# One search moved across the attention of a two-layer streaming encoder: seven bits ahead of the first recurrence tile instead of four, none beside the attention

## The chip, the cores and the metric

The kernel runs on one core of one Trainium2 chip. The metric is the device time of one execution in microseconds; the median of three executions of the kernel before is 2104.66 us.

## The reference, cut to what matters

The model has two layers. Each layer normalises its tokens, projects them, and runs four groups of heads over them: HGRN2 and retention (two gated linear recurrences), forgetting attention ("fox") and DSA sparse attention. It is done for 1040 prompt tokens and for 32 tokens of a running stream with 1024 cached rows. Only the DSA selection matters for the change: each query keeps the 256 keys with the highest index score.

```python
def _dsa_attend(q, k, v, iq, ik, iw, cid_q, cid_k, k_top):
    sc = jnp.einsum('bqhd,bkd->bqhk', iq, ik).astype(jnp.float32)
    score = jnp.einsum('bqhk,bqh->bqk', jax.nn.relu(sc), iw.astype(jnp.float32)) * IDX_SCALE
    adm = cid_k[None, :] <= cid_q[:, None]
    score = jnp.where(adm[None], score, -jnp.inf)
    kk = min(k_top, k.shape[1])
    _, sel = lax.top_k(score, kk)
...
    s = jnp.einsum('bqhd,bqsd->bqhs', q, k_sel).astype(jnp.float32) * (HD_C ** -0.5)
    s = jnp.where(valid[:, :, None, :], s, -jnp.inf)
    p = jax.nn.softmax(s, axis=-1).astype(v.dtype)
    return jnp.einsum('bqhs,bqsd->bqhd', p, v_sel)
```

## The kernel before, in words

The prompt is cut into nine tiles of 128 tokens (tile 0 is short and holds the stream's 32 tokens and the 16 meta tokens). A layer is one block of five instruction streams (PE, ACT, DVE, POOL, SP), each written out in a fixed order; they meet only at semaphores, and an engine that waits holds back all that is written behind the wait. The stages of a layer, for DVE:

1. **Norm, first projection and index scores.** DVE accumulates the index scores of eight units: the stream ("s", 32 x 1056) and the prompt tiles 2 to 8 (128 rows by 320, 448, ... 1088 keys), L1766.
2. **The selection's threshold.** No sort is used. The 256th largest score of each row is found bit by bit, 31 bits from bit 30 down. `search(n)` (L1810) makes n *steps* of it; a bit is `SEARCH` = 10 steps: one that sets the trial threshold `theta` (L1817), eight counts of the scores at or above it, one for each unit (`count_one`, L1783), and one that takes the bit over into `prefix` (L1822, L1824, L1826). A count writes the comparison's result, which nobody reads, to a scratch tile (`relu[0]`) and the sum into `cnt8`. Of the 31 bits four are made ahead of the first recurrence tile (`search(4 * SEARCH)`), then 7 steps in the first recurrence tile and 15 in each other, then what is left but two bits after the last tile (`search(31 * SEARCH - LATE - at_search[0])`), while PE still projects.
3. **The recurrence**, nine tiles of a chain between PE, ACT, DVE and POOL. For a tile POOL first turns and scales the loaded rows (`rotate` and `forget`, L2115 to L2136), ACT takes the logarithm, PE sums it up (L1031) and transposes (L1038), and DVE copies that out of PSUM (`x_qke`, L1840); all later work of the tile on DVE stands behind this copy. Between these PE fills its time with matmuls of the projections (L927), by a planner's table that the change does not touch.
4. **The attention**, 74 jobs in the order of the list `AJ`: 37 of fox, then 37 of DSA; a job is one head of one tile (the stream's is one job for all heads). PE makes the scores (L1221), DVE takes each row's maximum (`mneg`, L2067), ACT the exponentials (L1645), PE transposes these (L1235), ACT and DVE copy them out (L1378), PE multiplies with the values (L1271) and transposes back (L1279), and DVE scales (L1991).
5. The output projection, norm and residual (L1291, L2235).

In the attention DVE has *extra steps* besides: the last two bits of the search (`LATE`, 20 steps), then `penalise`, six steps for each of the eight units, which turn threshold and scores into an additive mask `pen` (0 or -1e30) that the DSA jobs add to their scores. By line: L1953 restores the sign, L1955 and L1956 compare above and equal, L1958 and L1959 rank the equal ones by a scan, L1961 and L1963 join, L1965 writes the mask. The extra steps stand in DVE's stream just ahead of the wait for a job's scores; how many ahead of which job comes from `steps_by`: in proportion to the jobs' lengths up to the job of DSA tile 6, and no later than `due`, four jobs ahead of the first job that reads the unit's mask. The 20 + 48 steps before are all made by job 61. The first late step waits for the last four stores of the projection (`st_out`), because from there on the scratch and masks lie where these stores read.

## Time and profile before

| | us |
|---|---|
| median of 3 runs | 2104.66 (2103.86 to 2107.75) |
| the profiled execution, its own time | 2108.83 |
| its span | 2107.0 |
| PE matmul busy | 1923.3 (91%) |
| DVE busy | 1387.2 (66%) |
| ACT busy | 736.7 (35%) |
| POOL busy | 254.4 (12%) |

Layer 1 fills the span up to about 1053 us, layer 2 the rest; they run the same instructions. In layer 1 the search begins at 182 us, the recurrence has DVE from 244 to about 545 us, the attention lasts from about 649 to 910 us, the output follows. In layer 2 all lies some 1051 us later. Granted clock 0.988 of full speed over the span.

### The profile page before, as it was taken

The numbers are of one execution on the slowest core, as the hardware profiler recorded it, in microseconds if no ns is written. First come the engines' busy times: TensorE is split into PE (matmuls) and PEld (weight loads), VectorE is DVE, ScalarE is ACT, GpSimd is POOL, SyncE is SP. The second block draws the span as 40 slices with busy tenths as digits, with TensorE's granted clock in tenths as the row PEclk, the third lists the DMA queues.
The fourth block names the chain that finished last, engine by engine and source line by source line (L and its number), as shares of the span: only waits on it lengthen the run. The fifth ranks groups of instructions, "written<-read, shape, count | busy, mean of one in ns | idle before, by whom it ended". The sixth has DMA issues, their size and how long they took to land. (4 is left out here: it accounts for less than half of the span.)

```text
span 2107.0 us, 27058 instructions
## 1 busy us (share of the span) xinstructions
PE 1923.3 (91%) x9670; PEld 1073.9 (51%) x9690; DVE 1387.2 (66%) x2961; ACT 736.7 (35%) x1678; POOL 254.4 (12%) x361
## 2 busy tenths in 40 slices
PE   7999999999998888999779999999999987889997
PEld 6434466555445556544364344665554455565443
DVE  4469398989796666542234693989888956674322
ACT  4451233423113444433244512434331134344332
POOL 0000223322100000001100002234221000000011
PEclk9999999999999999999979999999999999999999
DMA  7102232130513002224251022331314130122242
GB/s 245 59 22 78 70 106 86 61 103 28 154 38 73 14 14 91 87 99 147 107 175 61 23 75 75 103 99 46 103 43 139 38 76 11 34 70 88 99 149 105
DMA packets 151156, 173.44 MB, mean 82 GB/s; under 512 B 71392, under 2 KB 106848, under 8 KB 150832
## 3 DMA queue, kind: packets, MB, share of 16 engines
q1 hardware_dynamic: 122960, 134.34, 20.4%
q10 hardware_dynamic: 28064, 37.38, 5.0%
q8 instruction: 78, 1.28, 0.2%
q14 instruction: 54, 0.44, 0.1%
HBM read 114.94 MB, written 62.24 MB: 84 GB/s over the span
## 5 line engine op out<-in xcount | busy, mean ns | idle before, releaser
L927 PE MATMUL ps<-wring,xnT_arena 128*128 128x512 f32 (+2 forms) x2304 | 920.3, 541 | 0.0
L927 PEld LDWEIGHTS ps<-wring,xnT_arena 128*128 128x128 f32 x2304 | 403.1, 191 | 355.7 <-issue 338.7
L1783 DVE TENSOR_SCALAR_CACHE_REDUCE arena<-arena,theta 32x1056 bf16<-32x1056 f32 x496 | 461.3, 979 | 2.3
L1414 ACT COPY arena<-ps 128x512 f32<-128x512 f32 (+3 forms) x144 | 75.3, 523 | 447.7 <-PE ps L927 414.1
L1291 PE MATMUL ps<-wring,xnT_arena 128*128 128x512 f32 x512 | 222.8, 593 | 0.0
L2067 DVE TENSOR_REDUCE mneg<-ps 128x1 f32<-128x192 f32 (+9 forms) x148 | 113.9, 770 | 84.6 <-PE ps L1223 82.1
L1291 PEld LDWEIGHTS ps<-wring,xnT_arena 128*128 128x128 f32 x512 | 95.9, 190 | 114.8 <-issue 114.8
L1067 PEld LDWEIGHTS ps<-arena 128*128 128x128 f32 x488 | 68.7, 190 | 103.5 <-DVE arena L1890 75.1
L1067 PE MATMUL ps<-arena 128*128 128x128 f32 x488 | 79.5, 286 | 35.9 <-DVE arena L1890 35.7
L2235 POOL TENSOR_TENSOR arena<-arena 128x1024 f32<-128x1024 f32 (+1 forms) x16 | 35.4, 2213 | 584.0 <-DVE arena L2008 397.5
L1378 ACT COPY xnT_arena<-ps 128x512 f32<-128x512 f32 (+3 forms) x84 | 39.0, 464 | 181.8 <-PE ps L1235 139.1
L1221 PE MATMUL ps<-xnT_arena,arena 128*128 128x512 f32 (+4 forms) x240 | 86.3, 475 | 14.8 <-DVE xnT_arena L1378 13.2
L1221 PE MATMUL ps<-arena 128*128 128x512 f32 (+4 forms) x240 | 92.6, 473 | 7.8 <-DVE xnT_arena L1378 6.7
L1890 DVE TENSOR_TENSOR arena<-o_bc,arena 64x128 f32<-64x128 f32 x244 | 95.7, 392 | 3.8
L1645 ACT ACTIVATE arena<-ps,mneg 128x576 f32<-128x576 f32 (+5 forms) x84 | 80.9, 963 | 25.1 <-DVE mneg L2067 24.4
L1378 DVE COPY xnT_arena<-ps 128x512 f32<-128x512 f32 x104 | 61.2, 605 | 38.7 <-PE ps L1271 20.4
L1766 DVE SCALAR_TENSOR_TENSOR arena<-arena,iw 32x1056 f32<-32x1056 f32 (+7 forms) x64 | 63.7, 996 | 27.8 <-ACT arena L1477 25.7
L1235 PE MATMUL ps<-cf,arena 128*128 128x128 f32 (+2 forms) x596 | 79.1, 273 | 1.0 <-ACT arena L1645 1.0
L1872 DVE COPY_PREDICATED arena<-cm,ps 128x256 f32<-128x256 uint8 x122 | 63.5, 521 | 23.6 <-PE ps L1067 22.4
L1848 DVE TENSOR_TENSOR arena<-arena 128x256 f32<-128x256 f32 x122 | 76.2, 635 | 2.7
L1548 ACT ACTIVATE arena<-arena 128x128 f32<-128x128 f32 x122 | 37.7, 309 | 106.5 <-DVE arena L1848 100.1
L1235 PEld LDWEIGHTS ps<-cf,arena 128*128 128x128 f32 (+2 forms) x596 | 63.9, 136 | 18.9 <-issue 12.8
(271 smaller groups left out, 2468.0 us busy)
## 6 DMA issues: line engine op xcount, KB each, us to landing
projected<-arena ACTq DMA_DIRECT2D x130, 256.0 KB, 2.0
wring<-in_w_in SPq DMA_DIRECT2D x16, 1024.0 KB, 7.8
o_bc<-projected SPq DMA_DIRECT2D x36, 384.0 KB, 3.7
wring<-in_w_in SPq DMA_DIRECT2D x6, 2048.0 KB, 9.0
arena<-residual SPq DMA_DIRECT2D x17, 512.0 KB, 5.1
arena<-in_x_prompt SPq DMA_DIRECT2D x16, 512.0 KB, 5.0
wring<-in_w_out SPq DMA_DIRECT2D x8, 1024.0 KB, 6.1
residual<-arena SPq DMA_DIRECT2D x16, 512.0 KB, 2.7
```

The lines of the kernel that those rows point to most:

```text
L927: o = mm(bank(pbank(k), 0, w_), xnT[:, c, t * P:(t + 1) * P], w, start=(c == 0), stop=(c == CH - 1))
L1067: o = mm(bank(level_bank(k), 2 * n_ * g, 2 * n_), keys[:, g * P:(g + 1) * P], queries[:, g].rearrange("p e n -> p (e n)"), start=True, sto ...
L1221: o = mm(ps[:, col:col + w], qt[:, h, :], kt[:, h if m == "fox" else 0, key:key + w], start=True, stop=not adds, skip_group_check=True)
L1235: o = tr(ps[0:w, 512 * tbank[a] + P * i:512 * tbank[a] + P * i + P], pbuf((m, u, h))[:, col:col + w], C("ident"))
L1291: o = mm(bank(OUT_BANK[t] + half), yT[t % 2][:, c, :], wring[:, c * D + 512 * half:c * D + 512 * half + 512], start=(c == 0), stop=(c == C ...
L1378: copy(ptile[pt_of[m, u, h]][:, 4 * g * P:4 * g * P + size], bank(tbank[a], 0, size)).then_inc(te, 1)
L1414: nc.scalar.copy(stage[s][:, 0:wide], bank(pbank(k), 0, wide)).then_inc(p_ev, 1)
L1645: A(pbuf((m, u, h))[:, 0:hi - lo], ps[:, base + lo:base + hi], ACT.Exp, bias=mneg[:, s:s + 1], accum_out=rsum[:, s:s + 1]).then_inc(a_exp, 1)
L1783: V.tensor_scalar(cmp_out[0][r, (i % 2) * WMAX:(i % 2) * WMAX + uw[u]], score[u][r], th_, 0.0, op, ALU.add, accum_out=into[r, i:i + 1]).th ...
L1848: V.tensor_tensor(dl[k[1] % 2].rearrange("p (b s) -> p b s", s=size), bv, bv[:, :, size // 2 - 1:size // 2].broadcast_to([P, 2 * P // size ...
L1890: V.tensor_tensor(QL[k[1] % 2][r, :, e, :].rearrange("p g (b i) -> p g b i", i=size // 2), cut_(QKA[:, 0])[r, :, :, size // 2:], cut_(E[k[ ...
L2067: V.tensor_reduce(mneg[:, s:s + 1], ps[:, base + lo:base + hi], X, ALU.max, negate=True).then_inc(a_max, 1)
```

## The change

The search makes 70 steps ahead of the first recurrence tile instead of 40. Inside the recurrence nothing moves. After the last tile all the rest is made, 113 steps instead of 123, and none beside the attention. There only the 48 penalty steps are left, which the same rule now spreads over the same jobs. The wait for the last stores, with a product `thr8` of eight columns, now heads `penalise`, which is called ahead of every job, also with 0 steps; as long as no penalty step has been made (`at_pen[0] == 0`) each call makes both.

```diff
-                    cmp_out = [relu[0].bitcast(BF16)]
+                    cmp_out = relu[0].bitcast(BF16)
...
-                    search(4 * SEARCH)
+                    search(7 * SEARCH)
                     dve.wait_ge(x_split, 1)
...
                     head_squares(NT - 1)
-                    LATE = 2 * SEARCH
-                    search(31 * SEARCH - LATE - at_search[0])
+                    search(31 * SEARCH - at_search[0])
...
-                    def late_search(n):
-
-                        if at_search[0] == 31 * SEARCH - LATE:
+                    def penalise(n):
+
+                        if at_pen[0] == 0:
                             for j in jobs[-len(st_out):]:
                                 dve.wait_ge(st_out[st_out_slot[j]], st_out_at[j])
-                            cmp_out[0] = keep_equal
-                        search(n)
-                        if at_search[0] == 31 * SEARCH:
                             V.tensor_tensor(thr8, prefix.bitcast(F32), sg8, ALU.mult).then_inc(dve_own, one_more(own))
                             dve.wait_ge(dve_own, own[0])
-
-                    def penalise(n):
-
                         for _ in range(n):
...
-                    total = LATE + PEN_STEPS * len(UNITS)
-                    due = {job_no["dsa", u, 0] - 4: LATE + PEN_STEPS * (i + 1) for i, u in enumerate(PEN_ORDER)}
+                    total = PEN_STEPS * len(UNITS)
+                    due = {job_no["dsa", u, 0] - 4: PEN_STEPS * (i + 1) for i, u in enumerate(PEN_ORDER)}
...
-                            for _ in range(further(n)):
-                                if at_search[0] < 31 * SEARCH:
-                                    late_search(1)
-                                else:
-                                    penalise(1)
+                            penalise(further(n))
                             dve.wait_ge(a_sc, a_sc_at[key])
```

Only DVE's stream changes. Ahead of the first recurrence tile, DVE, the difference at the end of the fourth bit (`arena` holds the scores and the scratch, `sel` the counts):

```order
 L1824 TENSOR_SCALAR bitv<-sel 128x8
 L1826 TENSOR_TENSOR prefix<-prefix,bitv 128x8
+L1817 TENSOR_SCALAR theta<-prefix 128x8
+L1783 TENSOR_SCALAR arena,sel<-arena,theta 32x1056
+L1783 TENSOR_SCALAR arena,sel<-arena,theta 128x320
+L1783 TENSOR_SCALAR arena,sel<-arena,theta 128x448
+L1783 TENSOR_SCALAR arena,sel<-arena,theta 128x576
+L1783 TENSOR_SCALAR arena,sel<-arena,theta 128x704
+L1783 TENSOR_SCALAR arena,sel<-arena,theta 128x832
+L1783 TENSOR_SCALAR arena,sel<-arena,theta 128x960
+L1783 TENSOR_SCALAR arena,sel<-arena,theta 128x1088
```

A bit of these twelve instructions is added three times in each layer; behind the third stands, as before, the copy L1840 of the first recurrence tile.

DVE at the head of the attention, before (L2067 is a job's maximum, L1378 a copy of transposed exponentials, L1982 the stream's scaling):

```order
L2067 TENSOR_REDUCE mneg<-ps 128x1
L1817 TENSOR_SCALAR theta<-prefix 128x8
L2067 TENSOR_REDUCE mneg<-ps 128x1
L1378 COPY xnT_arena<-ps 128x512
L1378 COPY xnT_arena<-ps 128x128
L2067 TENSOR_REDUCE mneg<-ps 128x1
L1783 TENSOR_SCALAR arena,sel<-arena,theta 32x1056
L1783 TENSOR_SCALAR arena,sel<-arena,theta 128x320
L2067 TENSOR_REDUCE mneg<-ps 128x1
L1378 COPY xnT_arena<-ps 128x512
L1977 RECIPROCAL rinv<-rsum 128x1
L1982 TENSOR_SCALAR o_bc<-ps,rinv 32x64 x4
```

And in the changed kernel, whose lines here are numbered 7 to 11 lower (L1936 is `thr8`, L2056 the maximum, L1946 the first penalty step, L1948 and L1949 the second):

```order
L2056 TENSOR_REDUCE mneg<-ps 128x1
L1936 TENSOR_TENSOR sel<-prefix,sel 128x8
L1946 TENSOR_SCALAR arena<-arena,sel 32x1056
L2056 TENSOR_REDUCE mneg<-ps 128x1
L1378 COPY xnT_arena<-ps 128x512
L1378 COPY xnT_arena<-ps 128x128
L2056 TENSOR_REDUCE mneg<-ps 128x1
L1948 TENSOR_SCALAR arena,sel<-arena,sel 32x1056
L1949 TENSOR_SCALAR arena<-arena,sel 32x1056
L2056 TENSOR_REDUCE mneg<-ps 128x1
L1378 COPY xnT_arena<-ps 128x512
```

Penalty steps stand where search steps stood, from the third job on, and fewer of them; `thr8` stands ahead of each of the first three jobs.

## Rows read from the trace of the kernel before

**Rows 1.** Busy by stretch: us, PE, PEld, DVE, ACT, POOL, clock, DMA share, GB/s.
```profile
655.00:868.00 213.00, 180.15 (x1398) 123.21 (x1406) 142.51 (x289) 96.27 (x257) 0.71 (x2) 1.00 0.21 56
1706.00:1919.00 213.00, 179.47 (x1385) 122.90 (x1382) 141.60 (x289) 96.21 (x256) 0.19 (x1) 0.99 0.20 55
868.00:888.00 20.00, 19.35 (x136) 12.20 (x137) 8.47 (x16) 10.93 (x23) 0.00 (x0) 1.00 0.12 26
770.00:790.00 20.00, 14.27 (x116) 8.53 (x114) 14.04 (x25) 8.31 (x16) 0.00 (x0) 1.00 0.09 19
890.00:910.00 20.00, 14.87 (x117) 9.09 (x116) 10.84 (x19) 11.17 (x17) 0.00 (x0) 0.94 0.26 93
```

**Rows 2.** Timeline of DVE at the first recurrence tile: start, us, instruction, [idle before, releaser].
```profile
244.36 0.69 DVE L1840 COPY o_bc<-ps 128x512 f32<-128x512 f32 x1 [29.50 <-PE ps L1038]
...
1295.18 0.69 DVE L1840 COPY o_bc<-ps 128x512 f32<-128x512 f32 x1 [29.15 <-PE ps L1038]
```

**Rows 3.** Timeline of DVE in layer 1, where two bits of the search begin.
```profile
190.21 0.17 DVE L1817 TENSOR_SCALAR theta<-prefix 128x8 int32<-128x8 int32 x1
...
198.44 0.17 DVE L1817 TENSOR_SCALAR theta<-prefix 128x8 int32<-128x8 int32 x1
```

**Rows 4.** Timelines of POOL and PE ahead of the first recurrence tile, layer 1.
```profile
231.54 1.09 POOL L2115 TENSOR_TENSOR arena<-o_bc,cf 128x512 f32<-128x512 f32 x1 [60.22 <-DMA o_bc<-projected]
...
237.77 0.53 POOL L2161 MEMSET arena<- 128x512 f32 x1
...
238.42 1.14 PE L1031 MATMUL ps<-cf,arena 128*128 128x128 f32 x4 [2.36 <-ACT arena L1494]
```

**Rows 5.** Timelines of POOL and DVE in the second recurrence tile.
```profile
276.13 0.73 POOL L2146 TENSOR_TENSOR arena<-arena 128x256 f32<-128x256 f32 x1
...
246.14 0.90 POOL L2146 TENSOR_TENSOR arena<-arena 128x256 f32<-128x256 f32 x1
...
276.00 1.06 DVE L1783 TENSOR_SCALAR_CACHE_REDUCE arena<-arena,theta 128x832 bf16<-128x832 f32 x1
```

**Rows 6.** Timeline of DVE, first instruction behind the search's end in both layers.
```profile
649.41 1.46 DVE L1362 COPY xnT_arena<-ps 65x512 f32<-65x512 f32 x2 [5.29 <-PE ps L1137]
...
1699.96 1.46 DVE L1362 COPY xnT_arena<-ps 65x512 f32<-65x512 f32 x2 [5.31 <-PE ps L1137]
```

**Rows 7.** DVE's groups by line from 662 to 862: count | busy us, mean ns | idle before.
```profile
L1783 DVE TENSOR_SCALAR_CACHE_REDUCE arena<-arena,theta 32x1056 bf16<-32x1056 f32 (+7 forms) x16 | 15.4, 984 | 0.1
L1959 DVE TENSOR_TENSOR_SCAN arena<-cb,arena 32x1056 f32<-32x1056 bf16 (+7 forms) x8 | 13.6, 1704 | 0.0
...
L1961 DVE SCALAR_TENSOR_TENSOR arena<-arena,sel 32x1056 bf16<-32x1056 f32 (+7 forms) x8 | 7.9, 991 | 0.1
L1955 DVE TENSOR_SCALAR_CACHE_REDUCE arena<-arena,sel 32x1056 bf16<-32x1056 f32 (+7 forms) x8 | 7.9, 983 | 0.1
L1956 DVE TENSOR_SCALAR arena<-arena,sel 32x1056 bf16<-32x1056 f32 (+7 forms) x8 | 4.8, 604 | 0.0
L1953 DVE TENSOR_SCALAR arena<-arena,sel 32x1056 f32<-32x1056 f32 (+7 forms) x8 | 4.8, 600 | 0.1
...
L1963 DVE TENSOR_TENSOR arena<-arena 32x1056 bf16<-32x1056 bf16 (+7 forms) x8 | 4.3, 538 | 0.0
L1965 DVE TENSOR_SCALAR arena<-arena 32x1056 bf16<-32x1056 bf16 (+7 forms) x8 | 2.8, 350 | 0.2
```

**Rows 8.** Chain of waits, shares by line: 1700 to 1760, then 1760 to 1820.
```profile
by line: DMA gpre<-projected 15.0%; DVE arena L1783 12.3%; PE ps L1271 10.1%; PE ps L1221 8.2%; issue 7.8%; DVE mneg L2067 7.4%; PE ps L1260 7.2%; PE ps L1137 5.1%; DVE xnT_arena L1378 4.4%; PE ps L1235 4.4%; PE ps L1151 2.9%; DVE o_bc L199
...
by line: PE ps L1221 19.2%; PE ps L1271 18.6%; issue 13.3%; PE ps L1235 9.3%; DVE arena L1959 5.9%; DVE mneg L2067 5.7%; DVE xnT_arena L1378 3.4%; PE ps L1151 3.0%; PE ps L1279 2.6%; DVE arena L1961 2.2%; DVE o_bc L1991 1.5%; DVE arena L195
```

**Rows 9.** Last store of the projection, the stores' time to landing, first maximum.
```profile
648.61 0.33 ACTq L1420 DMA_DIRECT2D projected<-arena  x1
...
projected<-arena ACTq DMA_DIRECT2D x130, 256.0 KB, 2.0
...
657.24 1.26 DVE L2067 TENSOR_REDUCE mneg<-ps 128x1 f32<-128x1056 f32 x1 [3.13 <-PE ps L1223]
```

More of the change, by code:

```diff
@@ L1782, in count_one @@
                             dve.wait_ge(dve_own, counted[i % 2])
-                        V.tensor_scalar(cmp_out[0][r, (i % 2) * WMAX:(i % 2) * WMAX + uw[u]], score[u][r], th_, 0.0, op, ALU.add, accum_out=into[r, i:i + 1]).then_inc(dve_own, one_more(own))
+                        V.tensor_scalar(cmp_out[r, (i % 2) * WMAX:(i % 2) * WMAX + uw[u]], score[u][r], th_, 0.0, op, ALU.add, accum_out=into[r, i:i + 1]).then_inc(dve_own, one_more(own))
                         counted[i % 2] = own[0]
```

## The prediction

> **What bounds the kernel now.** I read the trace in four steps. First the busy time by stretch [rows 1]: over most of a layer PE is full, but in the attention, 655 to 868 us, it works 180.15 of 213 us and idles for 32.9 (33.5 in layer 2), and nobody else is full either: DVE works 142.5 us, ACT 96.3. Such a stage is bound by the chain from engine to engine: scores, maximum, exponentials, transposes, copies, values. A DVE instruction that stands ahead of a maximum can lengthen this chain although DVE has idle time elsewhere. Second DVE's timeline at the first recurrence tile [rows 2]: there DVE sits idle for 29.50 us in layer 1 and 29.15 us in layer 2, until a PE transpose of that tile is done. Third the end of the search, ahead of the attention: DVE is done with its search and waits another 5.3 us in both layers [rows 6], so what stands there is hidden behind PE. Fourth the chain of waits in the attention of layer 2 [rows 8]: the counts of the late search hold 12.3% of the first 60 us, which is 7.4 us; in the next 60 us the scan of the penalty steps holds 5.9%, 3.5 us. So the extra steps do stand on the path there, but by no means all the time.
>
> **Seven bits ahead of the recurrence: 0 us.** A bit takes 198.44 - 190.21 = 8.23 us from one theta to the next [rows 3]. Three added bits are 24.7 us in each layer, and the idle gap that they fall into is 29.50 and 29.15 us [rows 2]; 4.8 and 4.5 us of it are left. The copy L1840 starts when PE releases it, as before. Behind it everything on DVE keeps its place, since 30 added steps are three whole bits and the 15 steps of each tile fall on the same units. The cover is this gap; if the three bits took over 29.15 us, each us more would delay the first tile by one, in each layer. What the trace of before does not show is POOL's preparation of the tile running beside counts; that is the rival on the other side, below. Its bounds are 0 and 7.9 us a layer; I take 0, by the nearest row [rows 5].
>
> **Ten steps fewer behind the last tile: 0 us.** One bit, 8.2 us, leaves a stretch at whose end DVE waits 5.3 us for PE anyway [rows 6]. That wait grows to about 13.5 us and nothing starts earlier.
>
> **The wait for the stores moves from the third job to the first: 0 us.** The last store is issued at 648.61 and such stores land in 2.0 us at the median, so at about 651; the first maximum, behind which the wait cannot hurt, starts at 657.24 and has waited 3.13 us for PE itself [rows 9]. Six us are left. With thr8 it is made three times instead of once; thr8 is of the size of theta, 0.17 us [rows 3], and the first two fall into idle time ahead of jobs whose scores are late. At most 0.3 us a layer, taken as 0.
>
> **Two bits fewer beside the attention: the only term.** They are 2 x 8.23 = 16.5 us of DVE work a layer (the 16 counts alone are 15.4 us [rows 7]). The seven large lines of the penalty steps stay: 13.6 + 7.9 + 7.9 + 4.8 + 4.8 + 4.3 + 2.8 = 46.1 us [rows 7]. How much of 16.5 us of DVE work does the attention give back? I bound it by two readings.
> - From idle time. Of the 32.9 us that PE idles in 655 to 868, part would be there without any extra steps. Where DVE has none left, 868 to 888, PE idles 0.65 us of 20 [rows 1]; tile 8 of DSA, also without extra steps, idles 5.1 of 20, about as much as tile 8 of fox with them, 5.7 [rows 1]. So without extra steps the 213 us would idle some 193 x 0.65 / 20 + 5.1 = 11.4 us. The rest, 21.5 us, I put down to 46.1 + 16.5 = 62.6 us of extra steps: 0.34 us for each us. For 16.5 us that is 5.7 us a layer.
> - From the chain. Counts hold 7.4 us of it in layer 2 [rows 8]. Taking them away can't shorten this chain by more than that and its small neighbours, since behind the chain lies the next one, so 7.4 us is the upper end. The lower end is 0: DVE idles between the jobs, and a step can slide there.
>
> What speaks for less than 5.7 is where the work goes from. Not the first jobs are relieved but all of them, a little: by the rule for the steps 21 stand ahead of job 22 and its forerunners before (20 of the search, 1 penalty), and 14 penalty steps now. A unit's six steps are on average 1704 + 991 + 983 + 604 + 600 + 538 + 350 ns = 5.8 us [rows 7], so 14 of them are 13.5 us or more, against 17.2 before. Only 3 to 4 us are gone by there, the other 13 over jobs 23 to 61. And the new ones are longer: a scan of 1.7 us where counts took 1.0 [rows 7]. I take 5.0 us a layer, 10 us in all.
>
> **Sum.** Against the profiled execution, 2108.8 - 10 = 2098.8 us. That execution lies 4.2 us above the median of the runs shown; against this median, 2104.7 - 10 = 2094.7 us. Differences under 0.2%, 4.2 us here, are about what a measurement of this kernel can't tell from no change.
>
> **Rivals.** (a) *The attention gives back less than 2 us a layer*, because the longer penalty steps now sit in the small first jobs and the chain through PE is as late as the one through DVE. For it: DVE idles a third of the stage; tile 8 of fox and of DSA idle alike with and without extra steps [rows 1]. Against it: the counts' 12.3% on the chain [rows 8]. Time about 2102.5.
> (b) *It gives back all that the chain shows*, 7.4 us a layer and some of the small steps at the bits' ends: 15 to 16 us, time about 2089. For it: those rows. Against it: a chain names the last wait only, and the next one may lie a few tenths behind.
> (c) *POOL is held up ahead of the first tile, and the kernel gets slower.* In layer 1 POOL runs nine instructions from 231.54 to 238.30, and PE idles 2.36 us for their result (over ACT) at 238.42 [rows 4]: they are on the path. Before, DVE was silent there; now the seventh bit runs over them, from 244.36 - 29.50 + 2 x 8.23 = 231.3 to 239.5. If each of the eight that read had to wait for a count, on average 0.98 us [rows 7], that were 7.9 us a layer, 15.7 in all, and with the 10 us gained the time would be 2110.4. It decides from 0.63 us an instruction upward (8 x 0.63 = 5). Against it: L2146 took 0.73 us where it ran over a count that was on from 276.00 to 277.06, and 0.90 us at another place [rows 5]. No slowing by a count is seen.
> The Trainium skill, "SBUF — State Buffer", section "Who interferes with whom", calls the port pair that DVE and GpSimd share an exclusive lock, and says that the loser fully blocks. By this headline alone rival (c) would be the forecast, at 2110. The same section excepts the scalar form that also writes out its accumulator, which is what a count is; read so it gives 0, and the trace agrees, with 0.73 us.
> (d) *The change doesn't do what it says*: the order of DVE shows that it does; no chance is kept for it.
>
> **Chances.** The forecast, 3 to 6.5 us a layer, 0.60; (a) 0.15; (b) 0.20; (c) 0.05. So faster by over 0.2%: 0.60 + 0.20 = 0.80; within 0.2%: 0.15; slower: 0.05. The range leaves out (c) and the ends of (a) and (b): from 2086, a little below (b) at 2089 for what the small steps and the medians may add, to 2103, just above (a).
>
> **What the changed profile would show.** DVE's idle time ahead of L1840 falls from 29.50 and 29.15 to about 4.8 and 4.5 us, and L1840 starts at 244.4 and 1295 as before; POOL's nine instructions still take 6.8 us and PE's wait of 2.36 us stays. The recurrence is the same to a us. DVE's wait at the end of the search grows from 5.3 to about 13.5 us. The attention has no L1783, DVE works about 16 us less in it, and PE idles about 28 us instead of 33; each layer ends some 5 us earlier. I am wrong if the idle time ahead of L1840 vanishes and the copy comes late, if the attention's length stays though its DVE work is 16 us less (then the counts were covered), or if it shrinks by over 8 us a layer (then the chain's shares were too small a bound).

## The result, and the profile after

| | before | changed |
|---|---|---|
| median, us (20 runs of each) | 2108.60 (2103.42 to 2111.81) | 2112.36 (2105.76 to 2118.11) |
| changed / before | | 1.0023 (95%: 1.0013 to 1.0033) |
| the profiled execution, its own time | 2108.83 | 2109.71 |
| its span | 2107.0 | 2107.9 |
| mean granted clock | 0.9870 (89 runs, those beside the experiments) | 0.9822 (20 runs) |

The changed kernel is slower, by 0.23% or 4.9 us (the two medians alone lie 3.8 us apart, the two means 4.8). The forecast was 2094.7 us, 10 us faster. The sign was wrong.

The page of the changed kernel: PE is busy 8.5 us longer with the same matmuls (the trace of the kernel before lacks 20 of their records), DVE as long as before, since the bits have only moved.

```profile
span 2107.9 us, 27104 instructions
...
PE 1931.8 (92%) x9690; PEld 1077.8 (51%) x9690; DVE 1387.9 (66%) x2965; ACT 737.5 (35%) x1678; POOL 254.5 (12%) x361
```

**What came out as forecast.** DVE's timeline of the changed kernel at the first recurrence tile and behind the search (to be read against [rows 2, 6]):

```profile
241.64 0.69 DVE L1840 COPY o_bc<-ps 128x512 f32<-128x512 f32 x1 [2.02 <-PE ps L1038]
...
646.74 1.46 DVE L1362 COPY xnT_arena<-ps 65x512 f32<-65x512 f32 x2 [13.61 <-PE ps L1137]
...
1294.38 0.69 DVE L1840 COPY o_bc<-ps 128x512 f32<-128x512 f32 x1 [3.86 <-PE ps L1038]
...
1699.15 1.46 DVE L1362 COPY xnT_arena<-ps 65x512 f32<-65x512 f32 x2 [13.55 <-PE ps L1137]
```

The three bits fit into the gap: DVE is still released by PE, with 2.02 and 3.86 us to spare, and at the search's end it waits 13.6 us. POOL's nine instructions ahead of the first tile, now beside the seventh bit, and PE's wait for them (against [rows 4]):

```profile
230.48 1.10 POOL L2104 TENSOR_TENSOR arena<-o_bc,cf 128x512 f32<-128x512 f32 x1 [59.89 <-DMA o_bc<-projected]
...
232.71 0.73 POOL L2109 TENSOR_TENSOR arena<-arena 128x256 f32<-128x256 f32 x1
...
236.73 0.52 POOL L2150 MEMSET arena<- 128x512 f32 x1
...
237.38 0.68 PE L1031 MATMUL ps<-cf,arena 128*128 128x128 f32 x4 [2.05 <-ACT arena L1494]
```

From 230.48 to 237.25 are 6.8 us, as before. In layer 1 the copy starts 2.7 us earlier than in the kernel before. That is not the change: PE's L1031 took 1.14 us there before [rows 4] and takes 0.68 now, the granted clock from 238 to 242 being 0.57 then and 1.00 now, and in e1, with the same seven bits in front, the low clock and the late copy (243.85) are back. So the front and the tail show no cost; e1 tests it. The profiled pair differs by only 0.9 us in all because of such differences: its two attentions are 4.8 us longer, as the table below shows, and the rest is 3.9 us shorter, 2.7 of it at this place.

**Where the time went.** Lines of the changed kernel's attention carry lower numbers: L1946 to L1958 are the penalty steps, L1952 the scan, L2056 the maximum. DVE's groups by line from 659 to 862 (against [rows 7]) have no count left, and the maxima wait 37.7 us, where L2067 waited 23.9; the eight scans take 13.6 us as before:

```profile
L2056 DVE TENSOR_REDUCE mneg<-ps 128x1 f32<-128x64 f32 (+9 forms) x64 | 45.8, 716 | 37.7 <-PE ps L1223 36.5 <-DVE arena L1949 0.2
```

Busy time by stretch, attention of both layers (columns as in [rows 1]):

```profile
652.00:865.00 213.00, 182.69 (x1391) 124.05 (x1392) 125.52 (x249) 96.25 (x257) 0.72 (x2) 0.98 0.20 53
1705.00:1918.00 213.00, 182.96 (x1376) 125.12 (x1370) 125.24 (x248) 95.50 (x255) 0.19 (x1) 0.96 0.19 50
```

DVE works 17.0 and 16.4 us less, as forecast, and PE idles 30.3 and 30.0 us instead of 32.9 and 33.5. That looks like the forecast, and yet the stage is longer. The reason is the seventh figure: the clock was 1.00 and 0.99 there before and is 0.98 and 0.96 now. PE's extra busy time is not work, it is the same work at the lower level.

To see where the stage loses, I follow the maxima, which have the same order in every variant. DVE's timeline of the changed kernel; the widths name the jobs (1056: the stream, 576: a head of tile 4; jobs are counted from 0):

```profile
654.51 1.26 DVE L2056 TENSOR_REDUCE mneg<-ps 128x1 f32<-128x1056 f32 x1 [2.58 <-PE ps L1223]
...
672.32 2.33 DVE L1952 TENSOR_TENSOR_SCAN arena<-cb,arena 32x1056 f32<-32x1056 bf16 x1
674.69 0.76 DVE L2056 TENSOR_REDUCE mneg<-ps 128x1 f32<-128x576 f32 x1
...
681.30 0.76 DVE L2056 TENSOR_REDUCE mneg<-ps 128x1 f32<-128x576 f32 x1 [0.34 <-PE ps L1223]
...
782.25 1.26 DVE L2056 TENSOR_REDUCE mneg<-ps 128x1 f32<-128x1056 f32 x1 [2.36 <-PE ps L1223]
...
798.27 2.15 DVE L1952 TENSOR_TENSOR_SCAN arena<-cb,arena 128x960 f32<-128x960 bf16 x1
...
800.46 0.76 DVE L2056 TENSOR_REDUCE mneg<-ps 128x1 f32<-128x576 f32 x1
...
811.27 0.76 DVE L2056 TENSOR_REDUCE mneg<-ps 128x1 f32<-128x576 f32 x1 [0.93 <-PE ps L1223]
```

The same view and places in the kernel before:

```profile
674.91 0.68 DVE L1783 TENSOR_SCALAR_CACHE_REDUCE arena<-arena,theta 128x448 bf16<-128x448 f32 x1
675.52 0.75 DVE L2067 TENSOR_REDUCE mneg<-ps 128x1 f32<-128x576 f32 x1
...
680.67 0.76 DVE L2067 TENSOR_REDUCE mneg<-ps 128x1 f32<-128x576 f32 x1
...
785.73 1.26 DVE L2067 TENSOR_REDUCE mneg<-ps 128x1 f32<-128x1056 f32 x1 [2.38 <-PE ps L1223]
...
801.21 0.81 DVE L1959 TENSOR_TENSOR_SCAN arena<-cb,arena 128x320 f32<-128x320 bf16 x1
...
802.06 0.76 DVE L2067 TENSOR_REDUCE mneg<-ps 128x1 f32<-128x576 f32 x1
...
811.02 0.76 DVE L2067 TENSOR_REDUCE mneg<-ps 128x1 f32<-128x576 f32 x1 [0.74 <-PE ps L1223]
```

Subtracting the first maximum (654.51 now, 657.24 before) from each, and the same in layer 2:

| from the first maximum to | before, layers 1 / 2 | changed | difference |
|---|---|---|---|
| job 8, width 576 | 23.43 / 24.20 | 26.79 / 28.64 | +3.4 / +4.4 |
| job 37, width 1056 | 128.49 / 129.27 | 127.74 / 130.50 | -0.8 / +1.2 |
| job 45, width 576 | 153.78 / 154.56 | 156.76 / 159.54 | +3.0 / +5.0 |
| the output projection, L1301 | 250.6 / 252.6 | 252.6 / 255.4 | +2.0 / +2.8 |

So the attention does gain where it was to gain, 4.1 and 3.2 us between jobs 8 and 37 and 1.0 and 2.2 us at the end (of the 2.2, some 1.3 is the kernel before losing time at a low clock of its own, at 1900 to 1904). But it loses 3.4 to 4.4 us ahead of job 8 and 3.7 us in each layer in jobs 37 to 45. In both losing stretches a wide scan now stands ahead of a maximum of a small tile: the stream's, 2.33 us, ahead of job 6, where a count of 0.68 us stood; unit 7's, 2.15 us, ahead of job 41, where the scan of the narrowest unit stood, 0.81 us. Behind each PE waits, and then runs slow. PE's timeline of the changed kernel:

```profile
676.72 2.10 PE L1271 MATMUL ps<-xnT_arena 128*64 128x128 f32 x20 [3.10 <-ACT ptile L1378]
...
806.60 2.26 PE L1271 MATMUL ps<-xnT_arena,arena 128*64 128x128 f32 x20 [1.71 <-ACT xnT_arena L1690]
```

and of the kernel before:

```profile
677.55 1.46 PE L1271 MATMUL ps<-xnT_arena 128*64 128x128 f32 x20 [1.27 <-ACT ptile L1378]
...
807.89 1.46 PE L1271 MATMUL ps<-xnT_arena,arena 128*64 128x128 f32 x20 [1.40 <-ACT xnT_arena L1690]
```

The same twenty matmuls took 1.46 us before and take 2.10 and 2.26. Busy by stretch in the changed kernel shows the clock there:

```profile
677.00:680.00 3.00, 3.00 (x23) 1.82 (x19) 0.64 (x2) 0.27 (x1) 0.00 (x0) 0.55 0.00 0
...
807.00:810.00 3.00, 3.00 (x21) 1.82 (x17) 0.60 (x2) 0.27 (x1) 0.00 (x0) 0.50 0.00 0
1730.00:1734.00 4.00, 4.00 (x23) 2.30 (x20) 1.18 (x2) 0.27 (x1) 0.00 (x0) 0.50 0.01 4
```

Granted 0.50 to 0.55 is the 1.2 GHz level. In the kernel before, at these places:

```profile
677.00:681.00 4.00, 3.45 (x34) 2.57 (x35) 2.37 (x8) 1.14 (x7) 0.00 (x0) 1.00 0.00 0
808.00:812.00 4.00, 3.95 (x37) 2.85 (x37) 1.51 (x4) 0.94 (x5) 0.00 (x0) 1.00 0.00 0
```

The attention of the changed kernel has seven such falls in the profiled execution (three in layer 1, four in layer 2); the one before had one, at 1900 to 1904. The Trainium skill, "TensorE: Matmul & The Clock Gate", section "The HAM clock gate", says that the array's clock is gated by how busy PE has been of late, at half or at full rate. The trace agrees in kind: 0.55 behind a wait of 3.10 us, 1.00 where that wait was 1.27. But the clock is also 0.50 behind a wait of 1.71 us (after one of 1.07 us shortly before), and stays at 1.00 behind 1.40 (after 0.62), so the length of the last wait alone does not tell a fall.

The chain of waits of 1700 to 1760 (against [rows 8]) has lost the 12.3% of the counts and got PE's own lines in their place: L1221 went from 8.2 to 17.2%, L1235 from 4.4 to 8.1%, and the scan has come in.

```profile
by line: PE ps L1221 17.2%; DMA gpre<-projected 14.2%; PE ps L1271 10.7%; PE ps L1235 8.1%; issue 7.3%; PE ps L1260 7.2%; PE ps L1137 5.0%; DVE mneg L2056 4.4%; DVE arena L1952 3.8%; PE ps L1151 2.9%; DVE xnT_arena L1378 2.6%; PE ps L1279 2
```

**The theory.** The change is two edits. It takes two bits out of the attention, and it hands the 48 penalty steps, which stood ahead of jobs 22 to 61, to a rule that spreads them from the first job on. The first gains, the second loses more. Rivals: the seven bits in front (or POOL there) cost something after all; the repeated `thr8` costs; the counts were covered and nothing was gained. The scans of one unit after the other stood ahead of these jobs:

| unit | s | 4 | 5 | 6 | 2 | 7 | 3 | 8 |
|---|---|---|---|---|---|---|---|---|
| before, and e2 | 24 | 28 | 33 | 36 | 41 | 48 | 54 | 59 |
| changed | 6 | 15 | 23 | 29 | 34 | 41 | 51 | 58 |
| e3 | 11 | 17 | 22 | 28 | 34 | 48 | 53 | 59 |
| e11 | 26 | 30 | 34 | 37 | 46 | 53 | 58 | 63 |

### The profile page after: what moved, and what is told of

Its sections match the earlier page's. It is cut to its first block and busy times, and to the rows that moved or that the text cites. A ratio compares the mean times of both kernels' runs of the same rounds, so it can differ in the third digit from the quotient of the medians.

```text
span 2107.9 us, 27104 instructions
## 1 busy us (share of the span) xinstructions
PE 1931.8 (92%) x9690; PEld 1077.8 (51%) x9690; DVE 1387.9 (66%) x2965; ACT 737.5 (35%) x1678; POOL 254.5 (12%) x361
## 5 line engine op out<-in xcount | busy, mean ns | idle before, releaser
L2056 DVE TENSOR_REDUCE mneg<-ps 128x1 f32<-128x192 f32 (+9 forms) x148 | 114.0, 770 | 110.1 <-PE ps L1223 107.9
L1378 ACT COPY xnT_arena<-ps 128x512 f32<-128x512 f32 (+3 forms) x84 | 39.0, 464 | 199.5 <-PE ps L1235 153.7
L1221 PE MATMUL ps<-arena 128*128 128x512 f32 (+4 forms) x240 | 94.2, 481 | 8.8 <-DVE xnT_arena L1378 8.8
L1221 PE MATMUL ps<-xnT_arena,arena 128*128 128x512 f32 (+4 forms) x240 | 89.0, 488 | 9.3 <-DVE xnT_arena L1378 7.8
L1378 DVE COPY xnT_arena<-ps 128x512 f32<-128x512 f32 x104 | 61.3, 605 | 44.1 <-PE ps L1271 24.6
L1235 PE MATMUL ps<-cf,arena 128*128 128x128 f32 (+2 forms) x596 | 81.9, 280 | 0.5 <-ACT arena L1645 0.5
L1984 DVE TENSOR_TENSOR o_bc<-ps,rinv 128x128 f32<-128x128 f32 (+1 forms) x72 | 20.9, 291 | 86.8 <-PE ps L1279 85.6
L1235 PEld LDWEIGHTS ps<-cf,arena 128*128 128x128 f32 (+2 forms) x596 | 66.5, 140 | 18.4 <-issue 12.1
```

The costliest lines, as they stand in the source:

```text
L1221: o = mm(ps[:, col:col + w], qt[:, h, :], kt[:, h if m == "fox" else 0, key:key + w], start=True, stop=not adds, skip_group_check=True)
L1235: o = tr(ps[0:w, 512 * tbank[a] + P * i:512 * tbank[a] + P * i + P], pbuf((m, u, h))[:, col:col + w], C("ident"))
L1378: copy(ptile[pt_of[m, u, h]][:, 4 * g * P:4 * g * P + size], bank(tbank[a], 0, size)).then_inc(te, 1)
L2056: V.tensor_reduce(mneg[:, s:s + 1], ps[:, base + lo:base + hi], X, ALU.max, negate=True).then_inc(a_max, 1)
```

## The experiments

All are timed in five rounds against the kernel before on the same chip. The diffs are against the changed kernel unless said otherwise.

| | median, us | before, us | ratio (95%) | mean clock |
|---|---|---|---|---|
| e1 | 2106.28 | 2105.69 | 1.0001 (0.9990 to 1.0012) | 0.9875 |
| e2 | 2100.93 | 2105.69 | 0.9976 (0.9966 to 0.9986) | 0.9866 |
| e3 | 2105.28 | 2105.69 | 1.0002 (0.9993 to 1.0011) | 0.9860 |
| e4 | 2132.54 | 2105.69 | 1.0132 (1.0119 to 1.0146) | 0.9770 |
| e5 | 2121.21 | 2110.15 | 1.0047 (1.0031 to 1.0064) | 0.9835 |
| e6 | 2112.23 | 2110.15 | 1.0006 (0.9993 to 1.0019) | 0.9842 |
| e7 | 2106.99 | 2110.15 | 0.9986 (0.9974 to 0.9999) | 0.9860 |
| e8 | 2114.95 | 2110.15 | 1.0019 (1.0009 to 1.0029) | 0.9811 |
| e9 | 2103.68 | 2106.88 | 0.9986 (0.9976 to 0.9996) | 0.9869 |
| e10 | 2118.16 | 2106.88 | 1.0054 (1.0040 to 1.0067) | 0.9813 |
| e11 | 2110.08 | 2106.88 | 1.0016 (1.0004 to 1.0027) | 0.9842 |
| e12 | 2100.03 | 2109.68 | 0.9955 (0.9940 to 0.9971) | 0.9882 |

### e1: the front alone

The kernel before with seven bits in front; the last two stay beside the attention.

```diff
-                    search(4 * SEARCH)
+                    search(7 * SEARCH)
```

> The kernel before with seven bits ahead of the first recurrence tile, and still two bits beside the attention; only the rest behind the last tile is shorter, by three bits. Theory P (the loss lies in where the penalty steps stand in the attention) expects the time of the kernel before, within 2 us: the idle gap of DVE ahead of the first tile shrinks from 29.5 to about 4 us, and nothing else moves. Theory F (the three added bits ahead of the recurrence cost something that the changed kernel's profile hides) expects the changed kernel's loss here too, 4 to 5 us over the kernel before.

1.0001: no difference, and its maxima, counted from the first, lie within 0.3 us of those before in both layers. The front and the shorter tail are free. All of the 0.23% belongs to the attention.

### e2: the two bits gone, the penalty steps where they stood

```diff
-                    total = PEN_STEPS * len(UNITS)
-                    due = {job_no["dsa", u, 0] - 4: PEN_STEPS * (i + 1) for i, u in enumerate(PEN_ORDER)}
+                    total = 20 + PEN_STEPS * len(UNITS)
+                    due = {job_no["dsa", u, 0] - 4: 20 + PEN_STEPS * (i + 1) for i, u in enumerate(PEN_ORDER)}
...
+                    steps_by = [max(s - 20, 0) for s in steps_by]
...
-                            penalise(further(n))
+                            if further(n):
+                                penalise(further(n))
```

> The changed kernel, with the penalty steps ahead of the same jobs as in the kernel before (the first at job 21) and thr8 made once; the two bits are gone from the attention and nothing stands in their place. Theory P expects it faster than the kernel before: the counts leave the first 21 jobs, no wide penalty step takes their place, about 2.5 to 5 us a layer, 5 to 10 us in all, so 0.2% to 0.5% faster. Theory R (taking DVE work out of the attention gives nothing back, because the chain through PE or PE's clock takes its place) expects the time of the kernel before or that of the changed one.

0.24% faster than before, and 0.47% (1.0023 / 0.9976), or 9.9 us, faster than the changed kernel (by the last maximum of each attention 3.9 and 4.4 us, 8.3 in all), with the same instructions on DVE but for the repeated `thr8`. Only the places differ. This is the main result. DVE's timeline (L2058 is its maximum):

```profile
654.33 1.26 DVE L2058 TENSOR_REDUCE mneg<-ps 128x1 f32<-128x1056 f32 x1 [3.13 <-PE ps L1223]
...
779.37 1.26 DVE L2058 TENSOR_REDUCE mneg<-ps 128x1 f32<-128x1056 f32 x1 [2.39 <-PE ps L1223]
...
804.67 0.76 DVE L2058 TENSOR_REDUCE mneg<-ps 128x1 f32<-128x576 f32 x1 [0.74 <-PE ps L1223]
```

Job 37 comes 125.04 us after the first maximum, 3.5 less than before, and job 45 after 150.34, 3.4 less; in layer 2 job 37 is 4.6 us earlier. The gain is complete by job 22, where the counts ended, and stays level up to job 37 in layer 2 and job 60 in layer 1. So the two bits held 3.5 and 4.6 us of the path. (Half a us up or down is already there at job 3, ahead of the counts; from job 3 on it is 4.0 in both layers.) Then a part is lost again, 1.6 us in layer 1, at job 61, and 3.2 in layer 2, most of it at jobs 38 and 39, each time where the clock falls. PE's timeline of e2, tile 6 of DSA:

```profile
844.53 3.44 PE L1271 MATMUL ps<-xnT_arena,arena 128*64 128x128 f32 x28 [2.58 <-ACT xnT_arena L1690]
```

and busy by stretch there, clock 0.57:

```profile
844.00:848.00 4.00, 3.47 (x29) 2.85 (x30) 1.57 (x3) 1.38 (x6) 0.00 (x0) 0.57 0.00 0
```

### e3: spread, but not into the short jobs

No step ahead of jobs 0 to 8 and 37 to 45; in between in proportion to the number of jobs.

```diff
+                    steps_by = [min(30, 30 * max(0, n - 8) // 28) if n < 46 else min(total, 30 + 18 * (n - 45) // 16) for n in range(len(AJ))]
...
-                            penalise(further(n))
+                            if further(n):
+                                penalise(further(n))
```

> The changed kernel with none of the penalty steps ahead of jobs 0 to 8 and 37 to 45, the short jobs of tiles 0 and 4, in which its profile lost 3.4 to 4.4 us and 4.6 to 4.7 us a layer against the kernel before: 30 steps are spread over jobs 9 to 36, 18 over jobs 46 to 61. Theory P expects PE's waits of 3.1 us ahead of L1271 in those jobs to be gone, and the attention 5 to 8 us a layer shorter than the changed kernel's, in all 6 to 12 us faster than the kernel before. Theory R expects within 2 us of the kernel before.

1.0002: 0.2% better than the changed kernel, not as good as e2. In layer 1 it is 2.2 us ahead of the kernel before by job 7. Against e2 it then loses 2.2 us from job 8 to 12, around the stream's scan (job 11), and 2.9 from job 16 to 18, around unit 4's (job 17). Keeping the steps out of the short jobs brings back 0.21% of the 0.47%; packed into the jobs behind them the wide steps cost there.

### e4: four bits in front

```diff
-                    search(7 * SEARCH)
+                    search(4 * SEARCH)
```

> The changed kernel with four bits ahead of the first tile, so that the tail behind the last tile has three bits more than the changed kernel and two more than the kernel before. DVE waited 5.3 us at the end of the tail before, and two bits are 16.5 us, so it should be 11.2 us late for the attention in each layer: about 22 us slower than the changed kernel. If other work hides behind that lateness (stores and loads landing meanwhile), less: from 14 us.

1.3% slower than before, 1.1% or some 23 us slower than the changed kernel. The three bits, 24.7 us a layer, then stand behind the last tile, where 13.6 us are free: 11.1 us a layer are over, 22 in all. The three bits in front are what makes room at the tail. PE waits for DVE there (PE's timeline of e4), where before DVE waited for PE:

```profile
660.83 3.39 PE L1137 MATMUL ps<-cf,arena 128*65 128x128 f32 x16 [10.24 <-DVE xnT_arena L1362]
```

### e5: idle matmuls against the clock's fall, first form

Matmuls whose result nobody reads, ahead of the values of the first two heads of tile 4 (in the traces each of them shows as two, so five as x10).

```diff
+                        if (u, hp_) == (4, 0):
+                            pe.wait_ge(a_ot, a_ot_at[PV[i - 1]])
+                            for _ in range(5 if m == "fox" else 3):
+                                mm(bank(7, 256, 256), C("ident"), cf[:, 0:256], start=True, stop=True, skip_group_check=True)
```

> The changed kernel with matmuls added whose result nobody reads (five of 128x256 ahead of the values of fox tile 4, heads 0 and 1, three ahead of those of DSA tile 4), in the stretches in which PE waited 3.1 and 1.7 us for the transposed exponentials and in which its clock fell to the lower level (clock 0.5 at 678 to 680 and at 807 to 810 us in layer 1, the like in layer 2). Theory C (part of the loss is PE's clock, which falls behind PE's longer waits) expects these two falls a layer to be gone and the kernel 3 to 7 us faster than the changed one, though PE has more work. Theory D (only the delay by the DVE steps counts, the clock is a symptom) expects the changed kernel's time or a little more.

Slower than the changed kernel by 0.24% (1.0047 / 1.0023). The PSUM bank that they write is free only after ACT's copy, and that came about as late as the data that PE waits for. They stood behind the wait, not in it, and ran at the low clock (PE's timeline of e5):

```profile
677.47 4.63 PE L1243 MATMUL ps<-cf 128*128 128x256 f32 x10 [2.91 <-ACT xnT_arena L1694]
682.03 2.15 PE L1275 MATMUL ps<-xnT_arena 128*64 128x128 f32 x20
```

It tells nothing on the clock's price; e9 is its mended form.

### e6 and e7: one scan more, at a small and at a large tile

e2 with one scan of 32 x 1056, whose result nobody reads, ahead of job 6 (e6) or 30 (e7).

```diff
+                            if n == 6:
+                                for j in jobs[-len(st_out):]:
+                                    dve.wait_ge(st_out[st_out_slot[j]], st_out_at[j])
+                                r, w = rows_of("s"), uw["s"]
+                                V.tensor_tensor_scan(ranks[r, 0:w], CB("oneb")[r].broadcast_to([r.stop, w]), CB("oneb")[r].broadcast_to([r.stop, w]), 0.0, ALU.mult, ALU.add).then_inc(dve_own, one_more(own))
+                                dve.wait_ge(dve_own, own[0])
```

> The kernel with the penalty steps at their old places, with one scan of 32 x 1056 added in each layer, of the form of the penalty's scan (about 2.3 us), ahead of the maximum of job 6 (fox, tile 4, head 2), where the changed kernel has the stream's scan; its result is not read. Theory P (a wide step costs its length and more where the jobs are short) expects 2 to 4 us a layer over the kernel without it, 4 to 8 us in all, with PE's wait ahead of L1271 near 3 us and a fall of the clock behind it. Theory R (the place is of no matter) expects the same from this run and from the next.

> The same scan, ahead of the maximum of job 30 (fox, tile 7, head 2) instead, a long job, on top of the penalty step there. Theory P expects less than at job 6: 0 to 1.2 us a layer, at most 2.5 us in all over the kernel without it. Theory R expects the same as at job 6.

Against e2's 0.9976: e6 lies 0.30% higher, e7 0.10%, of which only the first is beyond the intervals. By the maxima just ahead of the scan and behind it the same scan costs 3.9 and 4.0 us a layer at job 6, and 1.8 in both layers at job 30. At job 6 it costs more than the 2.35 us that it takes. DVE's timeline of e6, then PE's:

```profile
674.96 2.35 DVE L2057 TENSOR_TENSOR_SCAN arena<-cb 32x1056 f32<-32x1056 bf16 x1
```

```profile
679.37 2.60 PE L1271 MATMUL ps<-xnT_arena 128*64 128x128 f32 x20 [3.05 <-ACT ptile L1378]
```

PE waits 3.05 us for it where it waits 0.65 in e2, and the twenty matmuls then take 2.60 us instead of 1.46:

```profile
673.98 1.46 PE L1271 MATMUL ps<-xnT_arena 128*64 128x128 f32 x20 [0.65 <-ACT ptile L1378]
```

So 2.4 us of waiting and 1.1 us of lower clock, 3.5 of the 3.9. This reproduces with one instruction the loss of the changed kernel ahead of job 8 (3.4 and 4.4 us). By the end of the attentions only 2.3 and 0 us of it are left in the profiled execution, because some falls of the clock that e2 has further on (job 61, and jobs 38 and 39 of layer 2) are missing there: a price read at one place need not reach the end in full.

### e8: thr8 once

```diff
-                            penalise(further(n))
+                            if further(n):
+                                penalise(further(n))
```

> The changed kernel, with thr8 and its wait made once instead of three times (penalise is not called with 0 steps). Both theories expect the changed kernel's time, within 1 us: 0.2 us of DVE work twice a layer, ahead of jobs whose scores are late.

1.0019 against the changed kernel's 1.0023, well within both intervals. The repeated `thr8` costs nothing.

### e9: idle matmuls into a free bank

As e5, but they wait only for what the values behind them wait for anyway, and write to a bank that is free.

```diff
+                        if (u, hp_) == (4, 0):
+                            evacuated(before[PV[i - 1]])
+                            for _ in range(5 if m == "fox" else 3):
+                                mm(bank(6, 256, 256), C("ident"), cf[:, 0:256], start=True, stop=True, skip_group_check=True)
```

> The changed kernel with the same idle matmuls as in the run before of this kind (five of 128x256 ahead of the values of fox tile 4, three ahead of those of DSA tile 4), but into unused columns of bank 6, for which PE need not wait for ACT's copy of the last output, so that they run inside PE's waits of 3.1 and 1.7 us and not behind them. Theory C (part of the loss is PE's clock, which falls behind these longer waits) expects the clock full at these places, two falls a layer fewer, and the kernel 3 to 7 us faster than the changed one. Theory D (the clock is a symptom and of no price) expects the changed kernel's time, at least as slow.

PE has 16 more matmuls, no other engine has less to do, every penalty step stands where the changed kernel has it, and it is 0.37% faster than that (0.9986 / 1.0023), 7.8 us. PE's timeline, then busy by stretch:

```profile
675.06 2.32 PE L1243 MATMUL ps<-cf 128*128 128x256 f32 x10
...
678.34 1.46 PE L1275 MATMUL ps<-xnT_arena 128*64 128x128 f32 x20 [0.95 <-ACT ptile L1382]
```

```profile
677.00:681.00 4.00, 3.05 (x28) 1.78 (x27) 1.67 (x6) 1.72 (x7) 0.00 (x0) 1.00 0.00 0
```

The wait of 3.10 us is now 0.95, the matmuls behind it take 1.46 again, the clock is 1.00, and the mean over the runs rises from 0.9822 to 0.9869. By the maxima the four places give back 1.1 and 1.6 us in layer 1 and 1.9 and 1.6 in layer 2 (jobs 7 to 8 and 44 to 45), 6.2 us; in the profiled execution 2.0 of them are lost again elsewhere. So the lower clock at these four places was most of the changed kernel's loss.

### e10: eight bits in front

```diff
-                    search(7 * SEARCH)
+                    search(8 * SEARCH)
```

> The changed kernel with eight bits ahead of the first recurrence tile. Of the gap ahead of L1840 the changed kernel left 2.02 us in layer 1 and 3.86 us in layer 2; one bit more is 8.2 us, so the first tile should start 6.2 and 4.4 us late. If the recurrence passes that on, 10.6 us slower than the changed kernel; if PE's fills take part of it up, from 3 us.

0.31% (1.0054 / 1.0023), 6.5 us, slower than the changed kernel. The gap is gone: in DVE's timeline the copy has no idle time ahead of it in either layer.

```profile
248.60 0.69 DVE L1840 COPY o_bc<-ps 128x512 f32<-128x512 f32 x1
...
1306.80 0.69 DVE L1840 COPY o_bc<-ps 128x512 f32<-128x512 f32 x1
```

With 2.02 and 3.86 us to spare, a bit of 8.23 is over by 6.2 and 4.4 us, 10.6 in all; 6.5 were paid. Seven is the most that the gap holds.

### e11: the penalty steps later still

e2, but spread up to the second head of tile 7 of DSA (job 65).

```diff
-                    last_job = job_no["dsa", UNIT_GROUPS[3][-1], H - 1]
+                    last_job = job_no["dsa", UNIT_GROUPS[4][-1], 1]
```

> The kernel with the penalty steps at their old places, but the spreading ends at job 65 (DSA tile 7, head 1) instead of 61, so that the same 48 steps are a little thinner and four long jobs share them. Theory P expects 0 to 3 us faster than with the old places; if the wide steps of tile 8's unit or tile 3's land ahead of a short job, 0 to 3 us slower.

0.4% slower than e2 (1.0016 / 0.9976), though the steps have more time. The rule now put a scan and the wide join behind it ahead of one maximum, at jobs 26, 53 and 58 (DVE's timeline of e11, L1954 is the join):

```profile
729.11 2.33 DVE L1952 TENSOR_TENSOR_SCAN arena<-cb,arena 32x1056 f32<-32x1056 bf16 x1
...
731.48 1.31 DVE L1954 SCALAR_TENSOR_TENSOR arena<-arena,sel 32x1056 bf16<-32x1056 f32 x1
...
732.82 1.16 DVE L2058 TENSOR_REDUCE mneg<-ps 128x1 f32<-128x960 f32 x1
```

3.6 us stand ahead of this maximum. From job 25 to 30 it goes from 0.6 to 6.9 us behind e2 in layer 1 and from 0.1 ahead to 5.4 behind in layer 2; 2.6 us of that come at job 26 in both, and the clock is at 0.50 behind it, at 735 to 741 us. That the pair is the reason was not tried apart, and another cause is not ruled out: in e2, the faster one, scan and join stand together too, ahead of jobs 33 and 36, the widest (1088). What is shown is that later is not better in itself.

### e12: the old places, and one filled wait

e2 with idle matmuls at the wait of 2.58 us shown there.

```diff
+                        if (m, u, hp_) == ("dsa", 6, 0):
+                            evacuated(before[PV[i - 1]])
+                            for _ in range(4):
+                                mm(bank(6, 256, 256), C("ident"), cf[:, 0:256], start=True, stop=True, skip_group_check=True)
```

> What the experiments so far point to, in one kernel: seven bits ahead of the recurrence and none beside the attention, the penalty steps at their old places, and four idle matmuls of 128x256 into unused columns of bank 6 ahead of the values of DSA tile 6, heads 0 and 1, the one place of that kernel's attention in which PE waited over 2 us (2.58 us) and its clock fell behind the wait, in both layers. Theory C expects these two falls to be gone and 2 to 4 us less than with the old places alone, so 7 to 9 us under the kernel before, ratio 0.9957 to 0.9967. Theory D expects the ratio of the old places alone, 0.9976, or slightly worse.

0.9955, 9.5 us faster than the kernel before and the best of all. PE's timeline, then busy by stretch: the 28 matmuls take 1.90 us instead of 3.44, at clock 1.00.

```profile
843.93 1.89 PE L1243 MATMUL ps<-cf 128*128 128x256 f32 x8
...
846.67 1.90 PE L1275 MATMUL ps<-xnT_arena,arena 128*64 128x128 f32 x28 [0.85 <-ACT xnT_arena L1694]
```

```profile
844.00:848.00 4.00, 3.15 (x33) 2.58 (x32) 3.68 (x6) 1.87 (x5) 0.00 (x0) 1.00 0.00 0
```

Its interval and e2's overlap a little (up to 0.9971, from 0.9966), so by the medians that the fill adds something is not settled. By the maxima it does: from job 60 to 61, where the filled wait is, e12 takes 1.6 us less than e2 in both layers, 3.2 in all. That it beats the kernel before is settled.

## Why the prediction was wrong

- **Seven bits ahead of the recurrence, 0 us: right** (e1 1.0001). 2.02 and 3.86 us were left, where 4.8 and 4.5 were forecast, and in e2 0.97 in layer 1; the margin moves with PE's clock ahead of the copy (full in the changed kernel, low before), and e10 shows that it was needed.
- **Ten steps fewer behind the last tile, 0 us: right.** The wait is 13.6 us; 13.5 was forecast.
- **The stores' wait and `thr8`, 0 us: right** (e8).
- **Rival (c), POOL held up by counts: refuted.** Nine instructions in 6.8 us, 0.73 us for one of them. The Trainium skill's exception in "SBUF — State Buffer", section "Who interferes with whom", which leaves the scalar form that also writes out its accumulator out of the operations that take the shared pair, agrees with that; its headline alone would have put 2110 here, close to the measured time and for a reason that does not hold.
- **Two bits fewer beside the attention, 5.0 us a layer: right in kind, too high in the sum.** With the places held (e2) the path is 3.5 and 4.6 us shorter by job 37, 4.0 in both layers from job 3 on. Over the kernel 5.1 us are left of it, because the clock then falls where it did not before. Both bounds of the prediction assumed that it stays as the rows of before had it, at 1.00 and 0.99.
- **The step that failed** is the next one, "What speaks for less than 5.7 is where the work goes from". I had seen that the penalty steps move into the first jobs and that "the new ones are longer: a scan of 1.7 us where counts took 1.0", and took 0.7 us a layer off for it. I reckoned with sums over many jobs, as if a us of DVE cost the same everywhere, and with the mean scan of 1.7 where the wide ones are 2.33 and 2.15. The runs show that the move is an edit of its own, worth 0.47% or 9.9 us against e2, twice the gain of the removal. One scan costs 3.9 us at job 6 and 1.8 at job 30 (e6, e7), and e11 loses 0.4% with the steps laid later still.
- **Rival (a)** named the cause, "the longer penalty steps now sit in the small first jobs", but ended it at no gain. For a loss a mechanism was missing: a scan that costs more than its own length, because PE's clock falls behind the wait that it causes. In e6 the wait was 2.4 us longer and the clock took 1.1 more. The chance of 0.05 for slower held only POOL's case.
- **What the changed profile would show.** DVE 16 us less in the attention: right. PE idle about 28 us: 30, and this figure hid the loss, since slower matmuls count as busy. "I am wrong if the attention's length stays though its DVE work is 16 us less": that came about, but the reason given for it, that the counts were covered, is not the one; e2 shows that they were not.

**The sum, in place of the forecast's -10.** The removal alone: -5.1 us (e2). The new places: +9.9. Together +4.8, and 4.9 were measured. (The 9.9 is the difference of the other two measurements, so the sum closes by itself and proves nothing more; each ratio is known to 0.1%, 2 us.) Filling PE's waits at four places gives back 7.8 (e9; 6.2 by the maxima there). The mean clocks give a second, rougher reading. Among the runs of one kernel, of those with ten runs or more, a clock lower by 0.001 goes with 1.2 to 2.2 us; the 0.0048 between 0.9870 and 0.9822 would then be 6 to 11 us, as an estimate. How far the two readings are the same microseconds stays open, since the idle matmuls also shift what follows. Open is also what decides whether the clock falls: at the head of DSA (786 to 790 in the changed kernel's profile) e2 has a fall in layer 2 and none in layer 1, with the same instructions.

## What to carry to other kernels

When work is taken out of a stage whose filler is dealt out by a rule, the rule deals the rest anew: hold the places first, measure the removal, and treat the new places as a change of their own. Price a filler step by the job that it stands ahead of, in microseconds and not in steps, the longest steps ahead of the largest jobs. Two wide steps ahead of one maximum may cost more than the two apart; e11 hints at it and does not show it. And read PE's busy time together with the granted clock: where the first rises and the second falls, the stage loses though its idle time shrinks.

## What the runs showed of the hardware that was not expected

- The granted clock went to 0.50 to 0.57 in an attention that keeps PE busy 85% of the time, behind waits of 1.7 to 3.1 us, and the matmuls behind them took 2.10 to 2.60 us instead of 1.46, or 3.44 instead of 1.90. Where such a fall was filled (e9 at job 45, e12 at job 61) the maxima came 1.6 us earlier each time.
- Sixteen matmuls of no use made a kernel 0.37% faster (e9); the same ones behind another wait made it 0.24% slower (e5).
- The scan takes 2.33 us for 1056 columns on 32 rows, 2.15 for 960 and 0.81 for 320 on 128: it goes by the columns, 2.2 to 2.5 ns each, where a maximum over 1056 columns takes 1.26 us.
